# Loads of the side-by-side retention and attention steps by token block, constants one block ahead, three steps among the last block's products

## The reference

```python
proj = h @ w_in[l]
aq, ak, av, rq, rk, rv, rg, ga, gr = jnp.split(proj, offsets, axis=-1)
att = sliding_window_attention(aq, ak, av, att_sinks[l])
ret = retention_chunkwise(rq, rk, rv)
ret = head_group_norm(ret, ret_gn_gain[l]) * silu(rg)
merged = sigmoid(ga) * (att @ w_att_o[l]) + sigmoid(gr) * (ret @ w_ret_o[l])
x = x + merged @ w_out[l]
# retention, one chunk of one head:
scores = einsum('bihd,bjhd->bhij', qi, ki) * decay_intra
o = einsum('bhij,bjhv->bihv', scores, vi) + einsum('bihd,bhdv->bihv', qi, state) * decay_q
state = decay_chunk * state + einsum('bjhd,bjhv->bhdv', ki * decay_k, vi)
```

## Time and profile before

| | us |
|---|---|
| median of 3 runs | 2707.33 |
| lowest, highest | 2704.08, 2710.63 |
| profiled execution | 2689.97 |
| its span | 2688.2 |
| TensorE busy in it | 2630.9 (98%) |
| VectorE, ScalarE, GpSimd busy | 1548.2, 1027.8, 1179.5 |

### The profile page before, as it was taken

The page is one execution under the profiler, slowest core; times in us unless marked ns, Lnnn a source line. Parts: engine busy times, 40 slices in busy tenths (PEclk is TensorE's granted clock), DMA queues, the critical chain, the costliest instruction groups (busy, mean ns, idle before and its releaser), DMA issues.

```text
span 2688.2 us, 35515 instructions
## 1 busy us (share of the span) xinstructions
PE 2630.9 (98%) x13170; PEld 2205.8 (82%) x13170; DVE 1548.2 (58%) x2628; ACT 1027.8 (38%) x2053; POOL 1179.5 (44%) x936
## 2 busy tenths in 40 slices
PE   7999999899999999999999999999999999999998
PEld 7788888677888988888888778989988888878886
DVE  4325555575434644554698641167647666668787
ACT  4122333475212423332444531057634322244443
POOL 2347878344425655565231763334234444300205
PEclk9999999899999999999999999999999999999999
DMA  4545766803542222222753344233043333273524
GB/s 169 181 184 204 266 228 249 305 1 122 199 169 90 79 86 79 79 86 71 274 184 99 114 153 142 74 69 65 20 141 100 104 114 106 95 257 133 188 95 164
DMA packets 161993, 372.35 MB, mean 139 GB/s; under 512 B 21365, under 2 KB 41973, under 8 KB 158197
## 3 DMA queue, kind: packets, MB, share of 16 engines
q1 hardware_dynamic: 161822, 370.08, 40.2%
HBM read 267.94 MB, written 101.83 MB: 138 GB/s over the span
## 4 chain that ended last, share of the span: by engine, by line
PE 88%; DVE 4%; POOL 2%; DMA 2%; ACT 2%; issue 1%; SPq 0%; POOLq 0%; DVEq 0%; ACTq 0%
PE PS L696 12%; PE PS L698 12%; PE PS L699 12%; PE PS L829 5%; PE PS L830 5%; PE PS L831 5%; PE PS L613 4%; PE PS L615 4%; PE PS L614 4%; PE PS L930 3%; PE PS L597 3%; PE PS L598 3%; PE PS L599 3%; PE PS L908 1%; PE PS L749 1%
## 5 line engine op out<-in xcount | busy, mean ns | idle before, releaser
L2094 POOL TENSOR_TENSOR WL<-WRAW,WH 128x512 fp32r<-128x512 f32 (+1 forms) x149 | 253.0, 1698 | 395.0 <-ACT WH L979 395.0
L696 PE MATMUL PS<-HH,WL 128*128 128x512 f32 (+1 forms) x928 | 349.0, 376 | 5.3 <-DVE HS L1736 3.1
L699 PE MATMUL PS<-HH,WH 128*128 128x512 f32 (+1 forms) x928 | 347.7, 375 | 0.0
L698 PE MATMUL PS<-HL,WH 128*128 128x512 f32 (+1 forms) x928 | 347.7, 375 | 0.0
L1428 DVE TENSOR_TENSOR WL<-TS,WH 128x512 fp32r<-128x512 f32 x216 | 227.5, 1062 | 182.9 <-ACT WH L979 182.8
L829 PE MATMUL PS<-WH,DAL 128*128 128x512 f32 x756 | 295.7, 391 | 5.5 <-DVE WL L1694 5.5
L830 PE MATMUL PS<-WL,DAH 128*128 128x512 f32 x756 | 294.7, 390 | 0.0
L831 PE MATMUL PS<-WH,DAH 128*128 128x512 f32 x756 | 294.6, 390 | 0.0
L2280 POOL TENSOR_TENSOR X<-X,DV 128x512 f32<-128x512 f32 x56 | 90.1, 1634 | 357.9 <-DVE DV L1806 275.3
L979 ACT ACTIVATE WH<-TS 128x512 fp32r<-128x512 f32 x216 | 130.9, 623 | 199.5 <-POOL TS L2110 199.4
L696 PEld LDWEIGHTS PS<-HH,WL 128*128 128x128 f32 x928 | 174.8, 188 | 37.1 <-DVE HS L1736 3.3
(11 more groups left out here) (366 smaller groups left out, 6145.1 us busy)
## 6 DMA issues: line engine op xcount, KB each, us to landing
WRAW<-in_u_f SPq DMA_DIRECT2D x56, 512.0 KB, 3.6
WRAW<-in_u_in SPq DMA_DIRECT2D x54, 512.0 KB, 4.4
WRAW<-scr_t SPq DMA_DIRECT2D x52, 512.0 KB, 3.7
scr_h<-HS SPq DMA_DIRECT2D x96, 256.0 KB, 2.2
WRAW<-in_u_gu SPq DMA_DIRECT2D x44, 512.0 KB, 3.5
scr_t<-TTa SPq DMA_DIRECT2D x19, 1024.0 KB, 4.4
WRAW<-in_u_out SPq DMA_DIRECT2D x24, 512.0 KB, 3.5
scr_x<-X SPq DMA_DIRECT2D x24, 512.0 KB, 5.0
```

The costliest lines, as they stand in the source:

```text
L696: e.matmul(PS[:, b, 0:wd], wl[:, blk(kk)], op_moving(q, kk, c0, wd, 0), start=(kk == 0), stop=False)
L698: e.matmul(PS[:, b, 0:wd], wh[:, blk(kk)], op_moving(q, kk, c0, wd, 1), start=False, stop=False)
L699: mm = e.matmul(PS[:, b, 0:wd], wh[:, blk(kk)], op_moving(q, kk, c0, wd, 0), start=False, stop=(kk == 3))
L2094: e.tensor_tensor(lo, raw, hi.bitcast(F32), ALU.subtract).then_inc(*c.inc("w_lo_p", i))
```

## The change

- The loads of `QK` and `AQ` are cut at token block 2: the first two token blocks are loaded by themselves, those of `AQ` to a new place `AQ0` in the low parts of P1's operand, those of `QK` for heads 2 and 3 to a new place `QX` in the low part of P7's operand (under RV of block 7, whose load waits for slot 7). `qk` and `queries` give the place.
- These loads are issued after P1 (`QK` heads 0 and 1, `AQ`) and P7 (RV 0, `QX`) of the last block, RV 1 after P2. All others follow P3.
- The constants are loaded after P5 of block 14. For that, one pair of down tiles moves to the late products, where five pairs stand at a distance of four products in place of five, and the sum one product behind the load in place of two.
- Slots 0, 1 and 2 stand in all four programs behind P5, P2 and P4 of block 15 (`EARLY_SLOTS`); the loop starts at slot 3. `LAG_A` is 3, so these three have no attention in them. The body of the loop becomes a function `slot`, else unchanged but for the waits for the constants, which now stand where these are used.
- The feed at slot 3, on all four engines, is gone; `SPARE` is empty.

```diff
+    AQ0 = at("AQ0", [P, 4, S], 100)
+    QX = at("QX", [P, 4, 256], B2 + 28)
...
-    N_RV, N_LATE = 5, 4
+    N_RV, N_LATE = 5, 5
     N_IN = NPAIR - 1 - N_RV - N_LATE
     T_LOAD = {EARLY[0]: 0, **{RVG[3 * g]: g + 1 for g in range(N_RV)},
               **{IN_ORDER[max(6 * g - 4, 0)]: g + 1 + N_RV for g in range(N_IN)},
-              **{LATE[5 * g]: NPAIR - N_LATE + g for g in range(N_LATE)}}
+              **{LATE[4 * g]: NPAIR - N_LATE + g for g in range(N_LATE)}}
     T_SUM = {EARLY[1]: 0, **{RVG[3 * g + 1]: g + 1 for g in range(N_RV)},
              **{IN_ORDER[6 * g + 2]: g + 1 + N_RV for g in range(N_IN)},
-             **{LATE[5 * g + 2]: NPAIR - N_LATE + g for g in range(N_LATE)}}
+             **{LATE[4 * g + 1]: NPAIR - N_LATE + g for g in range(N_LATE)}}
     T_STORE = {EARLY[2]: 0, **{RVG[3 * g + 2]: g + 1 for g in range(N_RV)},
                **{IN_ORDER[6 * g + 5]: g + 1 + N_RV for g in range(N_IN)},
-               **{LATE[5 * g + 3]: NPAIR - N_LATE + g for g in range(N_LATE)}}
+               **{LATE[4 * g + 2]: NPAIR - N_LATE + g for g in range(N_LATE)}}
 
     def t_set(g):
 
...
-        return c.at(("lg0", "lg1", "lm0", "lm0")[t] if t < 4 else "lm1", "aq")
+        return c.at("lg0" if t < 2 else "lm0" if t < 4 else "lm1", "aq")
+
+    def queries(j, t):
+
+        return AQ0[:, j, blk(t + 2)] if t < 2 else AQ[:, j, blk(t)]
+
+    def qk(n, t):
+
+        return QX[:, n - 4, blk(t)] if n >= 4 and t < 2 else QK[:, n, blk(t)]
 
     def qk_in(h, t):
 
-        return c.at(f"lga{2 * (h // 2) + t // 4}", "qk")
+        return c.at(f"lga{2 * (h // 2) + (t > 1)}", "qk")
 
     def hs(half):
         return slice(half * 512, half * 512 + 512)
...
-    LAG_A = 2
+    LAG_A = 3
+    SPARE = ()
+    EARLY_SLOTS = {"P5": 0, "P2": 1, "P4": 2}
...
+                    if lay == 0 and m == NB0 - 1 and p in EARLY_SLOTS:
+                        slot(EARLY_SLOTS[p])
...
+        for s in range(len(EARLY_SLOTS), n1 + LAG_A + 3):
+            slot(s)
...
-            if s == 3:
-                feed(("P3", 0, NB0 - 1, 0))
+            if s in SPARE:
+                if n_split[0] < len(ops) and ready(n_split[0], ("P3", 0, NB0 - 1, 0)):
+                    split()
...
-        w.wait_ge(*c.at("decays", "all"))
...
+                w.wait_ge(*c.at("decays", "all"))
...
-        def load_qk(n, half):
-            e.dma_start(QK[:, 4 * n:4 * n + 4, hs(half)],
-                        scr_qk[4 * n:4 * n + 4].rearrange("n p s -> p n s")[:, :, hs(half)]).then_inc(
-                            *c.inc(f"lga{2 * n + half}", "qk", 16))
+        def load_qk(n, late):
+            cols = slice(256, S) if late else slice(0, 256)
+            dst = QX[:, :, :] if n and not late else QK[:, 4 * n:4 * n + 4, cols]
+            e.dma_start(dst, scr_qk[4 * n:4 * n + 4].rearrange("n p s -> p n s")[:, :, cols]).then_inc(
+                *c.inc(f"lga{2 * n + late}", "qk", 16))
 
         def load_rv(t):
             e.dma_start(RV[:, t, :], scr_v[t]).then_inc(*c.inc(f"x{t}", "rv", 16))
 
-        def load_aq(name, lo, hi):
+        def load_aq(name, dst, lo, hi):
             cols = slice(128 * lo, 128 * hi)
-            e.dma_start(AQ[:, :, cols], scr_aq.rearrange("j p s -> p j s")[:, :, cols]).then_inc(*c.inc(name, "aq", 16))
+            e.dma_start(dst, scr_aq.rearrange("j p s -> p j s")[:, :, cols]).then_inc(*c.inc(name, "aq", 16))
+
+        def load_constants():
+
+            for g in (NPAIR - N_LATE - 2, NPAIR - N_LATE - 1):
+                w.wait_ge(*c.at(f"ts{t_set(g)}", ("out", g)))
+            e.dma_start(DECT[:, :, :], a["c_dect"]).then_inc(*c.inc("decays", "t", 16))
+            e.dma_start(DECQ[:, :, :], a["c_decq"]).then_inc(*c.inc("decays", "bias", 16))
+            e.dma_start(AB[:, :, :], a["c_ab"]).then_inc(*c.inc("decays", "all", 16))
 
         def first_loads(p):
 
             w.wait_ge(*bk.full((p, 0, NB0 - 1, 0)))
             if p == "P1":
-                for g in (NPAIR - N_LATE - 2, NPAIR - N_LATE - 1):
-                    w.wait_ge(*c.at(f"ts{t_set(g)}", ("out", g)))
-                e.dma_start(DECT[:, :, :], a["c_dect"]).then_inc(*c.inc("decays", "t", 16))
-                e.dma_start(DECQ[:, :, :], a["c_decq"]).then_inc(*c.inc("decays", "bias", 16))
-                e.dma_start(AB[:, :, :], a["c_ab"]).then_inc(*c.inc("decays", "all", 16))
                 stored0(3)
                 load_qk(0, 0)
-            elif p == "P7":
                 w.wait_ge(*c.at("gs_0", FILLS[-2]))
                 w.wait_ge(*c.at("gs_1", FILLS[-1]))
+                load_aq("lg0", AQ0[:, :, 256:512], 0, 2)
+            elif p == "P7":
                 load_rv(0)
+                load_qk(1, 0)
             elif p == "P5":
                 for q in QUARTERS:
                     w.wait_ge(*c.at(f"h{q}_0", (0, NB0 - 2)))
                 e.dma_start(AK[:, :], scr_ak[:, :]).then_inc(*c.inc("xr0", "ak", 16))
                 e.dma_start(AV.rearrange("p t c -> p (t c)"), scr_av[:, :]).then_inc(*c.inc("xr1", "av", 16))
             elif p == "P2":
-                load_qk(1, 0)
-            elif p == "P4":
                 load_rv(1)
-            elif p == "P3":
-                load_aq("lg0", 0, 1)
-                load_aq("lg1", 1, 2)
-                load_aq("lm0", 2, 4)
-                load_rv(2)
-                load_rv(3)
 
         for m in range(NB0):
             for x, (p, q) in enumerate(PROD):
@@ -2587,14 +2628,21 @@
                 elif m > 0:
                     feed(BEHIND[key][1])
                 down_tiles(key)
+                if m == NB0 - 2 and p == "P5":
+                    load_constants()
                 if m == NB0 - 1:
                     first_loads(p)
         load_qk(0, 1)
         load_qk(1, 1)
-        load_aq("lm1", 4, 8)
+        load_rv(2)
+        load_aq("lm0", AQ[:, :, 256:512], 2, 4)
+        load_rv(3)
+        load_aq("lm1", AQ[:, :, 512:S], 4, 8)
         for t in range(4, NT):
+            if t == NT - 1:
+                w.wait_ge(*bk.full(("rt", 7)))
+                w.wait_ge(*c.at("r_q", 7))
             load_rv(t)
-        feed(("P3", 0, NB0 - 1, 0))
```

More of the change, by code:

```diff
@@ L775, in pe_program, with slot @@
         nr, n1 = len(R1), len(A1)
-        for s in range(n1 + LAG_A + 3):
+        def slot(s):
             a = s - LAG_A
@@ L2205, in pool_program @@
                                 ALU.mult).then_inc(*c.inc("a_sc1", q))
-            if s == 3:
-                feed(("P3", 0, NB0 - 1, 0))
+            if s in SPARE:
+                if n_split[0] < len(ops) and ready(n_split[0], ("P3", 0, NB0 - 1, 0)):
+                    if on_pool(n_split[0]):
+                        split(n_split[0])
+                    n_split[0] += 1
+        for m in range(NB0):
+            for p, q in PROD:
+                key = p, 0, m, 0
+                down_sums(key)
+                if m == 0:
+                    i = n_split[0]
+                    if ops[i][0] == "B11":
+                        sums_of_tiles(i)
+                    if on_pool(i):
+                        split(i)
+                    n_split[0] += 1
+                else:
+                    feed(BEHIND[key][0])
+                if m == NB0 - 1 and p in EARLY_SLOTS:
+                    slot(EARLY_SLOTS[p])
+        for s in range(len(EARLY_SLOTS), n1 + LAG_A + 3):
+            slot(s)
         for i in range(16):
```

200 lines of the change are left out of this document (98 added, 102 removed).

## The result

Before: median 2704.19 us (2690.17 to 2715.18, 20 runs). After: 2692.14 us (2685.86 to 2701.72, 20 runs). The ratio is 0.9967, 95% interval 0.9953 to 0.998. The change is faster by 9 us by the ratio and 12 by the medians; 10.8 was forecast. The forecast median of 2696.5 was set against the 2707.33 of three runs, and twenty give 2704.19.

The account below looks back on a forecast made before the run. TensorE, 98% busy, was taken as the bound, with gain only in waits and slow clock at the join. Of at most -15.5 us (-8.3, -7.2), -10.8 remained, other terms 0: 2707.33 to 2696.5 us, own range 2692 to 2700, full range 2688 to 2706.

Parts of the forecast that it names:

- The waits for QK and AQ: At the join of last in-projection products and slots, four TensorE idle times go with earlier loads: -8.3 us.
- The store as the next wait: First attention step's L1602 waits for the last block's store, issued at 500.8, landing in 2.4 us; TensorE then idles 1 and 1.6.
- VectorE's pace: After the store, VectorE and not TensorE sets the pace of the first attention steps, 2.95 us each.
- The clock stays up: At the join the 1.2 GHz stretches go, at most -7.2 us; clock at 1.00 from 495 to 530 us.
- rival 2: Clock falls again at about 506 us for some 14 to 18 us; saving 4 to 5.5, 2702.5 us; chance 0.19.
- Slots 0 to 2 between the products: About 3.0 us of TensorE work moves ahead of P3 without shrinking; with no cover it costs 1 us.
- The rest of the slots: From slot 3 to the slots' end, less retention, a wait for ON and longer PT waits sum to 0, range -1 to +1.5.
- The weight splits: Slot 3's splits and three RO weight loads move behind the first AO product: price 0, without that cover 1.2 us.
- The fifth late pair: A down-tile pair moved to the late products fits beside busy TensorE: price 0, at most 2 us.
- Rival 1: TensorE keeps its own pace in the first attention steps; the whole 15.5 us is saved, 2691.8 us; chance 0.12.
- rival 3: Loads fail: RV0 lands late or the last store takes 9.0 us; saving 4 to 7.5, 2701.5 us; chance 0.13.
- rival 4: Slower: store takes 9.0 us, clock falls, sparse slots keep 1.2 GHz longer; +5 or more, say 2714 us; chance 0.06.

Follow-up runs that it names:

- e2: Changed kernel with the loads alone: no early slots, LAG_A back at 2; 2697.19 us, ratio 0.9969 to the kernel before.
- e8: As e2 (loads alone, lag 2), with two AO products moved among the last slots; 2695.96 us, ratio 0.9978 to the kernel before.
- e10: Changed kernel with four late pairs and the constants loaded in the last block again; 2704.73 us, ratio 1.0001 to the kernel before.
- e1: The changed kernel run and profiled once more, unedited; 2695.75 us, ratio 0.9965 to the kernel before.
- e9: Changed kernel with idle identity products on TensorE at the slots' end and ahead of the second attention stage; 2691.31 us, ratio 0.9954 to the kernel before.
- e6: Changed kernel with only slots 0 and 1 early and LAG_A back at 2; 2697.27 us, ratio 0.9979 to the kernel before.
- e3: Changed kernel with the feed at slot 3 put back on all four engines; 2698.03 us, ratio 0.9971 to the kernel before.
- e11: Candidate: changed kernel's loads, no early slots, lag 2, idle TensorE products, output-stage splits and loads behind the slots' loop; 2684.01 us, ratio 0.9939 to the kernel before.
- e4: Changed kernel with the first three probability tiles written to another place, free of the stores; 2687.75 us, ratio 0.9945 to the kernel before.
- e12: Changed kernel with output-stage weight splits and loads behind the slots' loop, loads spread over AO steps; 2695.9 us, ratio 0.9974 to the kernel before.
- e7: As e2 (loads alone, lag 2), with the feed put at slot 10; 2696.86 us, ratio 0.9981 to the kernel before.

## Why the prediction was right, point by point

**The waits for QK and AQ, -8.3.** Right. No idle time between 495 and 530 us is released by a load.

**The store as the next wait.** Right in place and size: issued at 500.17 (forecast 500.8), landing in 2.8 us (2.4), L1582 at 503.18 (503.2). The waits behind it were 1.32 and 1.36 us (1.0 and 1.6). That the size came out is in part luck: the same store took 4.2 and 6.1 us in e2 and e8, whose joins are alike. Named against the change was a rule of the Trainium skill, page DMA: Bandwidth & Descriptors, section Queues, rings and completion order, by which a semaphore's increment lands only after every earlier write of its engine. The trace of the changed kernel gave it nothing to hold up, since the late loads stand behind the store. In e10, where 1.5 MB stand ahead, QK landed 2.8 us later, which fits the rule; whether it is the order or only the amount of data, no run tells.

**VectorE's pace, 2.95 us a slot.** Nearly right: the steps of L1582 are 2.87, 2.85 and 3.31 us apart, 9.03 in all against 8.85. The prediction read the 2.90 of the earlier trace rows as taken at full clock, though by its own reckoning the clock came back only at 521.4, between the two steps; the steps of 2.87 and 2.85 show that the size was right even so.

**The clock stays up.** Wrong in part, and this is rival 2 in small. It fell at about 506.6 and was back at about 510. In this profile the first wide product came 0.7 us after the forecast (514.57, forecast 513.9). In the profiles of e1 and e9, whose join has the same instructions, the same fall lasts longer: the slices from 505 to 520 us hold 3.4 us of half clock here, 6.8 in e1 and 10.2 in e9, and the wide product comes 1.0 and 3.1 us later. VectorE's pace hides a short fall in part, and a longer one less. The Trainium skill, page TensorE: Matmul & The Clock Gate, Part 1, calls the number of slow matmuls at a kernel's start run-variable. The traces show the like here, in the middle of a kernel, by these three numbers.

**Gain at the join, -10.8.** 44.85 to 35.20 is -9.65; at AO it is -8.9. Of it the loads bring all: 33.02 in e2 and 35.04 in e8, by whether the clock fell.

**Slots 0 to 2 between the products, neutral.** Held on the scale of a microsecond: e2, without them, reaches AO 1.5 us earlier, but with no fall of the clock at the join, and e8, with one, has the wide product level. The text followed only the changed kernel, never the loads alone, and so did not see that one of its parts was worth nothing.

**The rest of the slots, 0 (-1 to +1.5).** From the wide product to AO, 122.24 us became 123.02: +0.8, with a fall of the clock in it.

**The weight splits, price 0, at most 1.2.** This step failed. AO to RO went from 43.66 to 48.15. Without the fall of the clock at its start e9 has 46.68 and e6 46.13, which makes 2.5 to 3.0 us for the moved splits and loads. With the fall, 48.15 and 48.43 stand against 46.16 in the second profile of before and 45.58 in e3: 2.0 to 2.9. The working looked at VectorE's idle time beside one AO product (1.37) and fitted one split of 1.23 into it. It left out what follows behind VectorE, on ScalarE and GpSimd, down to RO. And it priced the three loads by when their weights are used, some 40 us later, and not by what stands behind them in SyncE's queue: the stores of TB took 4.5 us instead of 3.2, and VectorE waited for them four times from 640 to 686 us, 12.3 us in all, against three times and 4.4 before. In the chain the stores weigh more than the splits, but no run moved the loads and the splits apart.

**The fifth late pair, 0.** Right as to TensorE: from 1600 to 1700 us it is never idle for long enough to show (20.00 of 20 in each stretch), and from RO to the first of the 128 WST products it is 1013.62 us against 1012.96. But the text took this part and the earlier constants as having no worth either. e10 says they are a condition of the early slots: without the two together 4.4 us are lost by AO. Its pairs and constants were not taken apart.

**The sum.** 12.05 us by the medians and 9.7 by the means of the 20 runs, against 10.8. The agreement is partly luck. From the first profile of before to that of after, -8.9 at AO become -4.4 at RO, by the moved splits and loads and because this profile of before kept the clock at the slots' end and that of after lost it. Against the second profile of before, which lost it too, the changed kernel's two profiles reach RO 9.3 and 8.1 us sooner. The granted clocks of the single runs say that the first was the rare case. So the gain of the means is what the distances give when like is set beside like: about half of it is shorter work and waits at the same clock, about half a higher clock, of which the join is a part. A further share of the 12 between medians is how the two groups of the changed kernel fell, 11 runs to 9. The fall at 1763, which the prediction did not have, makes those groups. Where the 83 runs of before lose the clock, two profiles can't tell. Rival 1 fell with the pace of L1582, rival 3 with the landings, rival 4 with the times.

## What to carry to other kernels

When a change pulls loads out of a queue's rush, ask of each of its parts what it is worth alone; here the order of the loads brought everything and the reordered products nothing that could be measured. Splits and loads that a change pushes behind a stage should be followed along their whole chain to the next stage, and into the queue that they share with that stage's stores, not fitted into one idle gap. Before two profiles are compared, see from the granted clock of all runs which kind of execution each of them is. Where times fall into groups, look for a short pause of TensorE followed by a long stretch at half clock: a few small products put into the pause took the fall away in the profiles and the slower group in the times.

## What the runs showed of the hardware

After a pause of 1.06 us came a stretch of some 27 us at half clock, but not in each execution. All kernels but e9 and e11 have that pause, before among them (TensorE's row in the changed kernel stands below). The profiles of after, e2, e3, e4, e8, e10 and e12 show the stretch; those of e1, e6, e7 and the two of before don't.

```profile
1760.81 1.30 PE L948 MATMUL PS<-V,PT 128*128 128x64 f32 x10 [1.06 <-DVE PT L2015]
```

In the changed kernel's profile TensorE was busy for the whole 25 us from 1765 to 1790 and stayed at 0.50. At the slots' end it came back at about 643, after 5.5 us of unbroken work, at the join after about 4. What differs between these stretches was not tried. In e9 and e11 nine products of 128 columns filled the pause, TensorE was busy for the whole 30 us from 1760 to 1790, and the clock stayed at 1.00.

Stretches at half clock cost unlike amounts. The 27 us with nothing else to wait for cost 12.7. At the join, where TensorE also waits for VectorE, 3.4 more us of half clock brought the wide product 1.0 us later (e1 against the first profile), and 6.8 more brought it 3.1 later (e9).

A store of 256 KB landed in 2.1 to 6.1 us at the join with the late loads behind it (e4 and e8), and in 9.0 in the old queue.
